# A two-block transformer layer on one core: squares read from PSUM by halves, the residual as one operation, and another order of work between the blocks

## The chip, the cores and the metric

The kernel runs on one core of one Trainium2 chip. The metric is the device time of one execution in microseconds (us), from runs of the whole program. Five engines work side by side, each through its own list of instructions in order: TensorE (PE, with its weight loads PEld), VectorE (DVE), ScalarE (ACT), GpSimd (POOL) and SyncE (SP, which here only issues DMA). They wait for each other on semaphores.

## The reference

Two blocks, one after the other, on 256 tokens of width 1024, in float32. The first is a hybrid attention layer, the second an attention layer with context and a mixture of experts. What the change touches is the seam between them:

```python
# end of the first block
m = jax.nn.sigmoid(gate_a) * (y_a @ w_a) + jax.nn.sigmoid(gate_b) * (y_b @ w_b)
return x + rms_norm(m @ w_o, norm_post)
...
# start of the second block: h is projected, hc is the context's
h = modulate(rmsnorm(x, norm_attn[l]), sh_a, sc_a)
hc = modulate(rmsnorm(xc, norm_attn[l]), csh_a, csc_a)
mix, mix_c = token_mixers(h, hc, rows, cols, w_in[l], ...)
```

`rms_norm` is y = x * rsqrt(mean(x * x) + 1e-6) times a gain. Inside `token_mixers`, h goes through w_in (1440 columns) and the compressed context through w_kv_up; then come attention, the router, and 16 experts whose weights are about half of all bytes read.

## The kernel before

**Data.** The tokens stand in two tiles of 128 (t = 0, 1), the width in halves of 512 (h = 0, 1). `xn` is the residual stream, `rn` holds rows (the output of w_o, later the normalised tokens), both 2 x 1024 columns.

**Groups.** The dense part of both blocks is a list of named groups, `DENSE` (line 96), and `schedule` (line 132) turns it into `SCHEDULE`, which PE, ACT and DVE each walk through in the same order. The name tells the work: `wo{t}{h}` is m @ w_o, `ckv{t}{h}` the context's keys and values, `hT{t}{h}` four transposes of normalised tokens, `xa{t}{h}` the projection by w_in (h = 2 is the last 416 columns), `bG`/`bF` spread a modulation row over all partitions, `modT2` turns the last modulation rows, `kc0` to `kc3` turn the context's keys, `lq`/`lk` turn the second block's latents.

**Two banks.** All these groups share two PSUM banks in turn (`BANK_OF`, line 109): a group gets the bank of the group two places ahead of it in the list, and PE waits at its start (`begin`, line 979) until ACT or DVE has released that bank (`leave`, line 513). So the order in the list also decides which copy PE waits for.

**Weights.** SP streams 2 MB slots of weights from HBM into the two halves of `ring` (and into `qk` for some), each when the previous user of the buffer is released (`released`, line 495). Float32 weights are split in a high part (ACT, line 650 through `copy`) and a low part (DVE, line 1724), in quarters: ACT waits until PE has finished with the same quarter of the weights before (`quarter_released`), DVE subtracts, PE starts. X2, X1, X0 are the thirds of w_in; `SPLIT_AFTER` (line 93) puts the four quarters of X2 behind hT01, modT2, bF1 and hT10.

**The seam.** For each `wo{t}{h}` ACT copies the bank to `rn`, which frees the bank. After the second half ACT squares and sums the row (`sum_squares`, line 655), DVE forms the mean, POOL raises it to the power -0.5 (line 952), DVE multiplies by root and gain (`block1_norm`, line 1601) and adds to `xn`. Then ACT squares `xn`, DVE and POOL form the second root and DVE writes the normalised tokens (`normalise`, line 1596), which `hT` turns. For t = 1 the squares of `xn` stand behind ckv11 on ACT, the rest behind hT01 on DVE.

## Time and profile before

| | us |
|---|---|
| median of 3 runs | 709.14 |
| lowest, highest | 708.98, 713.59 |
| the profiled execution | 711.06 |
| its span, first to last instruction | 709.3 |
| PE busy in it | 594.4 (84%) |
| DVE, ACT busy | 301.8, 225.8 |
| end of wo11 on PE (first block's last product) | 296.38 |
| start of xa02 (second block's first projection) | 317.50 |
| start of the second block's attention on PE | 376.09 |

The profiled execution is 1.9 us above the median. A row of the timeline gives start, duration, engine, line, operation, what it writes and reads, and in brackets how long its engine was idle before it and who ended that.

### The profile page before, as it was taken

Reading aid. Unit: us, or ns where it says so; the run is one execution under the profiler, and the core shown is the slowest. Engines: PE = TensorE matmul, PEld = TensorE weight load, DVE = VectorE, ACT = ScalarE, POOL = GpSimd, SP = SyncE. Lnnn points to the kernel's source line nnn. Section 1 sums busy time; section 2 is a strip of 40 time slices with the busy share of each in tenths; the row PEclk is TensorE's granted clock in tenths of the full one; section 3 lists DMA queues with packets and bytes.
Section 4 is the critical chain, followed back from the end, with each engine's and each line's share of the span. In section 5 each row is a group of like instructions: output and inputs, shape, how many; then the busy total and the mean of one; then the engine's idle time right before and its main releaser. Section 6 shows DMA issues by size and latency. Waiting matters only on the chain.

```text
span 709.3 us, 8571 instructions
## 1 busy us (share of the span) xinstructions
PE 594.4 (84%) x3373; PEld 366.7 (52%) x3373; DVE 301.8 (43%) x743; ACT 225.8 (32%) x485; POOL 17.6 (2%) x34
## 2 busy tenths in 40 slices
PE   3999999999998979969998999977995775656553
PEld 2998977778766748638654444436331311211011
DVE  5355576666664462473737876144210100000005
ACT  5244354445334233465235656111010100010001
POOL 3000000000000001000000000000000000000000
PEclk9999999999999999999999999996997798889787
DMA  8774867657688592355476001754899999999992
GB/s 320 258 254 151 326 237 280 267 215 290 262 328 347 237 369 106 118 179 207 147 305 260 1 1 66 290 201 185 335 430 426 426 424 430 427 427 428 423 414 90
DMA packets 19080, 193.00 MB, mean 272 GB/s; under 512 B 3296, under 2 KB 4576, under 8 KB 7264
## 3 DMA queue, kind: packets, MB, share of 16 engines
q1 hardware_dynamic: 15584, 188.49, 66.3%
q10 hardware_dynamic: 3168, 2.39, 1.1%
q0 software_dynamic: 288, 1.57, 0.5%
q8 instruction: 27, 0.44, 0.2%
q14 instruction: 13, 0.11, 0.0%
HBM read 190.87 MB, written 1.05 MB: 271 GB/s over the span
## 4 chain that ended last, share of the span: by engine, by line
PE 61%; DMA 24%; DVE 7%; ACT 3%; issue 2%; POOL 0%; SPq 0%; ACTq 0%; POOLq 0%; DVEq 0%
PE bank L1009 25%; DMA qk<-in_stream 17%; DMA ring<-in_stream 6%; PE bank L986 5%; PE bank L997 5%; PE bank L1495 3%; PE bank L1407 3%; PE bank L1253 3%; PE bank L1370 3%; PE bank L1338 2%; PE bank L1442 2%; PE bank L1335 2%; PE bank L1280 2%; DVE weight_parts L1724 2%; PE bank L1533 1%
## 5 line engine op out<-in xcount | busy, mean ns | idle before, releaser
L1009 PE MATMUL bank<-weight_parts,u_parts 128*128 128x512 f32 (+2 forms) x416 | 125.5, 384 | 3.7 <-ACT rows L650 1.2
L1724 DVE TENSOR_TENSOR weight_parts<-ring,weight_parts 128x1024 fp32r<-128x1024 f32 (+2 forms) x68 | 78.0, 1181 | 47.9 <-ACT weight_parts L650 45.8
L1009 PEld LDWEIGHTS bank<-weight_parts,u_parts 128*128 128x128 f32 x416 | 75.7, 188 | 20.9 <-issue 2.1
L650 ACT ACTIVATE weight_parts<-ring 128x1024 fp32r<-128x1024 f32 (+2 forms) x68 | 68.1, 1024 | 28.5 <-PE bank L1009 27.5
L1009 PE MATMUL bank<-u_parts,weight_parts 128*128 128x256 f32 x256 | 50.7, 293 | 4.6 <-DVE x_parts L1775 3.1
L1009 PE MATMUL bank<-weight_parts,x_parts 128*128 128x512 f32 (+1 forms) x128 | 48.3, 377 | 0.0
L1009 PEld LDWEIGHTS bank<-u_parts,weight_parts 128*128 128x128 f32 x256 | 42.0, 198 | 6.8 <-issue 4.7
L986 PEld LDWEIGHTS bank<-ident,sp 128*128 128x128 f32 (+1 forms) x218 | 26.1, 140 | 24.3 <-DVE sp L2016 15.7
L1009 PE MATMUL bank<-x_parts,weight_parts 128*128 128x256 f32 x128 | 37.0, 289 | 0.0
L986 PE MATMUL bank<-ident,sp 128*128 128x128 f32 (+1 forms) x218 | 32.1, 274 | 3.8 <-DVE sp L2016 1.9
L701 ACT ACTIVATE sp<-sp,small 128x128 f32<-128x128 f32 (+1 forms) x48 | 21.3, 444 | 35.8 <-DVE small L1685 35.8
L2123 DVE TENSOR_TENSOR sp<-sp,bank 128x512 f32<-128x512 f32 x4 | 2.8, 689 | 61.0 <-PE bank L1495 61.0
L2134 DVE COPY pt<-bank 128x512 f32<-128x512 f32 x4 | 2.8, 692 | 56.7 <-PE bank L1533 56.7
L1495 PE MATMUL bank<-ring,tz 128*32 128x512 f32 x128 | 19.9, 758 | 8.1 <-DMA ring<-in_stream 8.1
L2121 DVE SCALAR_TENSOR_TENSOR sp<-sp,bank 128x512 f32<-128x512 f32 x4 | 2.8, 688 | 55.9 <-ACT sp L916 55.9
L1009 PEld LDWEIGHTS bank<-weight_parts,x_parts 128*128 128x128 f32 x128 | 24.0, 188 | 4.5
L1495 PE MATMUL bank<-parts,tz 128*32 128x512 f32 x128 | 17.7, 682 | 10.1 <-DMA parts<-in_stream 10.1
L884 ACT ACTIVATE tz<-bank,small 128x128 f32<-128x128 f32 x16 | 6.0, 455 | 62.8 <-PE bank L1442 62.8
L1009 PEld LDWEIGHTS bank<-x_parts,weight_parts 128*128 128x128 f32 x128 | 25.3, 198 | 0.0
L650 ACT ACTIVATE mo<-bank 128x512 f32<-128x512 f32 (+3 forms) x22 | 12.0, 544 | 39.1 <-PE bank L1009 20.3
L650 ACT ACTIVATE pt<-bank 128x384 f32<-128x384 f32 (+1 forms) x18 | 9.2, 512 | 47.5 <-PE bank L1533 47.5
L997 PE MATMUL bank<-ring,lat 128*128 128x512 f32 (+2 forms) x56 | 23.0, 556 | 1.3 <-DVE tz L1593 0.8
(289 smaller groups left out, 994.7 us busy)
## 6 DMA issues: line engine op xcount, KB each, us to landing
ring<-in_stream SPq DMA_DIRECT2D x44, 2048.0 KB, 9.2
parts<-in_stream SPq DMA_DIRECT2D x12, 2048.0 KB, 35.5
qk<-in_stream SPq DMA_DIRECT2D x10, 2048.0 KB, 12.9
tabs<-in_stream SPq DMA_DIRECT2D x5, 2048.0 KB, 35.4
mo<-in_stream SPq DMA_DIRECT2D x5, 2048.0 KB, 38.6
vvc<-in_stream SPq DMA_DIRECT2D x5, 2048.0 KB, 39.2
tz<-in_stream SPq DMA_DIRECT2D x5, 1024.0 KB, 38.0
lat<-in_stream SPq DMA_DIRECT2D x5, 1024.0 KB, 40.1
```

What stands on the lines that cost most here:

```text
L650: ins = act.activation(dst, src, ACT.Copy, scale=scale)
L701: ins = act.activation(k, k, ACT.Exp, bias=nm[:, u % 2, 2 * b + q:2 * b + q + 1], accum_out=sums[:, u, 2 * b + q:2 * b + q + 1])
L986: return pe_.transpose(dst, src, ident[0:n, 0:n])
L997: ins = pe_.matmul(o, lhs(c), rhs(c), start=(c == 0), stop=(c == chunks - 1))
L1009: ins = pe_.matmul(o, lhs(a, c, i), rhs(b, c, i), start=(c == 0 and n == 0), stop=(c == chunks - 1 and n == 2))
L1253: ins = pe_.matmul(MB[32 * j:32 * j + 32, :], csil[:, c, :], w[:, k, 512 * j:512 * j + 512], start=(c == 0), stop=(c == KC - 1), tile_posi ...
L1280: pe_.matmul(SB[0][:, :], q[:, P:S], k.rearrange("p g s -> p (g s)"), start=True, stop=True)
L1335: ins = pe_.matmul(o, qwT[:, j, q * P:(q + 1) * P], kP[:, b, :], start=True, stop=True)
L1370: ins = pe_.matmul(OB[p % 2][HD * b:HD * b + HD, 0:S], v, pT[p % 2][:, b, i, :], start=(i == 0), stop=(i == 3), tile_position=(0, HD * b))
L1407: ins = pe_.matmul(D_(name)[:, :], oT[:, c, t * P:(t + 1) * P], w[:, c, :], start=(c == 0), stop=(c == KC - 1))
L1495: ins = pe_.matmul(bank[b][32 * e:32 * e + 32, :], xs[:, g % 2, c, e * CAP:(e + 1) * CAP], w[e][:, k, :], start=(c == 0), stop=(c == KC - ...
L1724: dve.tensor_tensor(quarter(weight_parts[:, SLOT:], name, q), quarter(slot(name), name, q), quarter(weight_parts, name, q).bitcast(F32), A ...
```

## The change

It does four things. (1) For each `wo{t}{h}`, ACT no longer copies: it squares and sums the half straight from PSUM (128x512), and DVE then multiplies the bank by the gain into `rn`, which now frees the bank (`post_gain`). (2) The root is applied together with the residual, one SCALAR_TENSOR_TENSOR for each half (`residual`), and the squares of `xn` are taken by halves. (3) The normalisation steps and the four quarters of X2's split become items of their own (`high`, `low`, `square`, `residual`, `mean`, `norm`) that the table `ACROSS` hangs behind wo01, wo11, ckv00 and ckv01. (4) The list is reordered: hT00, hT01 stand ahead of the ckv groups, hT10, hT11 right behind them, then xa02; the groups modT2, bG, bF and kc go in between the xa groups. A table of names replaces the counted squares. The instructions of PE are the same, in another order.

```diff
-SPLIT_AFTER = {"hT01": "X2", "modT2": "X2", "bF1": "X2", "hT10": "X2"}
...
-         "mT11", "modT1", "wo00", "cc0", "cc1", "wo10", "clT", "wo01", "wo11", "ckv00", "ckv01",
-         "ckv10", "hT00", "hT01", "ckv11", "bG0", "bG1", "modT2", "bF1", "bF0", "hT10", "hT11",
-         "kc0", "kc1", "kc3", "xa02", "kc2", "xa12", "xa01", "xa11", "xa00", "lq0", "lq1",
-         "xa10", "lk0", "lk1", "qu00", "qu01", "xkv00", "xkv01", "qwT0", "qu10", "qwT1", "kwT",
+         "mT11", "modT1", "wo00", "cc0", "cc1", "wo10", "clT", "wo01", "wo11", "hT00", "hT01",
+         "ckv00", "ckv01", "ckv10", "ckv11", "hT10", "hT11", "xa02", "kc0", "xa12", "modT2", "kc1",
+         "xa01", "bG0", "bG1", "xa11", "kc2", "bF1", "kc3", "bF0", "xa00", "lq0",
+         "xa10", "lq1", "lk0", "lk1", "qu00", "qu01", "xkv00", "xkv01", "qwT0", "qu10", "qwT1", "kwT",
...
+ACROSS = {"wo01": [("high", 0), ("residual", 0), ("square", 0), ("high", 1), ("mean", 0), ("low", 0), ("norm", 0)],
+          "wo11": [("high", 2), ("low", 1), ("residual", 1)], "ckv00": [("square", 1), ("mean", 1), ("low", 2), ("norm", 1)],
+          "ckv01": [("high", 3), ("low", 3)]}
...
+                elif kind == "high":
+
+                    arrived(eng, "X2")
+                    quarter_released(eng, X2_SPLIT - 1, n)
+                    copy(quarter(weight_parts, "X2", n), quarter(slot("X2"), "X2", n)).then_inc(split_a, 1)
+                elif kind == "square":
+                    for h in range(2):
+                        eng.wait_ge(x1_ready, 2 * n + h + 1)
+                        sum_squares(xn[:, n, 512 * h:512 * h + 512], 10 + n if h else 8 + n, sp[:, 0:512])
...
-                        copy(rn[:, t, 512 * h:512 * h + 512], D_(name)[:, :], name)
-                        if h == 1:
-                            kept(eng, f"wo{t}0")
-                            kept(eng, name)
-                            sum_squares(rn[:, t, :], 4 + t, sp[:, 0:D])
-                            if t == 0:
-
-                                eng.wait_ge(x1_ready, 1)
-                                sum_squares(xn[:, 0, :], 8, sp[:, 0:D])
+                        sum_squares(D_(name)[:, :], 14 + t if h else 4 + t, sp[:, 0:512])
...
-                        if name == "ckv11":
-                            eng.wait_ge(x1_ready, 2)
-                            sum_squares(xn[:, 1, :], 9, sp[:, 0:D])
...
-            def block1_norm(t):
-
-                mean_root(4 + t, 1, D, 5 + 2 * t)
+            def post_gain(t, h):
+
+                name = f"wo{t}{h}"
+                filled(eng, name)
                 eng.wait_ge(post_in, 16)
-                own(dve.scalar_tensor_tensor(rn[:, t, :], rn[:, t, :], rs[:, 4 + t:5 + t], post, ALU.mult, ALU.mult))
-                dve.tensor_tensor(xn[:, t, :], xn[:, t, :], rn[:, t, :], ALU.add).then_inc(x1_ready, 1)
-                eng.wait_ge(x1_ready, t + 1)
+                cols = slice(512 * h, 512 * h + 512)
+                eng.wait_ge(squares, squared(name))
+                leave(dve.tensor_tensor(rn[:, t, cols], D_(name)[:, :], post[:, cols], ALU.mult), name)
...
+                elif kind == "residual":
+                    eng.wait_ge(roots, n_mean[0])
+                    for h in range(2):
+                        kept(eng, f"wo{n}{h}")
+                        x = xn[:, n, 512 * h:512 * h + 512]
+                        dve.scalar_tensor_tensor(x, rn[:, n, 512 * h:512 * h + 512], rs[:, 14 + n:15 + n], x, ALU.mult, ALU.add)\
+                           .then_inc(x1_ready, 1)
+                elif kind == "mean":
+                    first_half(8 + n, squared(f"x{n}0"))
+                    half_mean(10 + n, 8 + n, squared(f"x{n}1"))
+                elif kind == "norm":
+                    eng.wait_ge(roots, n_mean[0])
+                    eng.wait_ge(x1_ready, 2 * n + 2)
+                    dve.tensor_scalar(rn[:, n, :], xn[:, n, :], rs[:, 10 + n:11 + n], None, ALU.mult).then_inc(normed, 1)
```

The first place is PE behind the last product of the first block, wo11. Names: rows are the tokens to turn (hT), `ring,lat` the context's products (ckv), `modr,lat` the spreads (bG, bF), `modr` alone modT2, `qk` the kc turns. Of the kernel before:

```order
L1009 MATMUL bank1<-weight_parts_64,ml_parts_67 128x512
L997 MATMUL bank0<-ring_49,lat_60 128x512 x2
L997 MATMUL bank1<-ring_49,lat_60 128x512 x2
L997 MATMUL bank0<-ring_49,lat_60 128x512 x2
L986 MATMUL bank1<-ident_61,rows_53 128x128 x4
L986 MATMUL bank0<-ident_61,rows_53 128x128 x4
L997 MATMUL bank1<-ring_49,lat_60 128x512 x2
L1183 MATMUL bank0<-modr_62,lat_60 128x512
L1183 MATMUL bank1<-modr_62,lat_60 128x512
L986 MATMUL bank0<-ident_61,modr_62 128x128 x4
L1183 MATMUL bank1<-modr_62,lat_60 128x512
L1183 MATMUL bank0<-modr_62,lat_60 128x512
```

Of the changed one, the same place on PE up to the first rows of xa02:

```order
L1017 MATMUL bank1<-weight_parts_64,ml_parts_67 128x512
L994 MATMUL bank0<-ident_61,rows_53 128x128 x4
L994 MATMUL bank1<-ident_61,rows_53 128x128 x4
L1005 MATMUL bank0<-ring_49,lat_60 128x512 x2
L1005 MATMUL bank1<-ring_49,lat_60 128x512 x2
L1005 MATMUL bank0<-ring_49,lat_60 128x512 x2
L1005 MATMUL bank1<-ring_49,lat_60 128x512 x2
L994 MATMUL bank0<-ident_61,rows_53 128x128 x4
L994 MATMUL bank1<-ident_61,rows_53 128x128 x4
L1017 MATMUL bank0<-weight_parts_64,u_parts_65 128x416 x2
```

The first ckv product now takes bank0 from hT00, where before it followed wo11 with a bank that had long been free, and the spreads and kc turns are gone from here.

The second place is PE at the end of xa12 and the start of xa01, in the changed kernel:

```order
L1017 MATMUL bank0<-weight_parts_64,u_parts_65 128x416 x2
L1017 MATMUL bank0<-weight_parts_64,hl_parts_68 128x416
L994 MATMUL bank1<-ident_61,modr_62 128x128 x4
L994 MATMUL bank0<-ident_61,qk_56 96x128 x4
L1017 MATMUL bank1<-weight_parts_64,u_parts_65 128x512 x2
```

and in the kernel before:

```order
L1009 MATMUL bank0<-weight_parts_64,u_parts_65 128x416 x2
L1009 MATMUL bank0<-weight_parts_64,hl_parts_68 128x416
L1009 MATMUL bank1<-weight_parts_64,u_parts_65 128x512 x2
L1009 MATMUL bank1<-weight_parts_64,hl_parts_68 128x512
L1009 MATMUL bank1<-weight_parts_64,u_parts_65 128x512 x2
```

Two short groups, modT2 and kc1, now stand between the two projections, and kc1 writes the bank that xa12 has just filled.

The third place is DVE over the first tokens, in the changed kernel, from the low parts of WO1 (the second weights of w_o) to the turned tokens (`weight_parts<-ring,weight_parts` with 2x416 columns is a quarter of X2):

```order
L1740 TENSOR_TENSOR weight_parts<-ring,weight_parts 128x1024 x4
L1616 TENSOR_TENSOR rows<-bank,vvc 128x512
...
L1751 SCALAR_TENSOR_TENSOR x_sb<-rows,small,x_sb 128x512 x2
L1581 TENSOR_SCALAR small<-small 128x1
L1621 SCALAR_TENSOR_TENSOR small<-small 128x1
L1744 TENSOR_TENSOR weight_parts<-ring,weight_parts 128x2x416
L1759 TENSOR_SCALAR rows<-x_sb,small 128x1024
L1616 TENSOR_TENSOR rows<-bank,vvc 128x512
L1621 SCALAR_TENSOR_TENSOR small<-small 128x1
L1744 TENSOR_TENSOR weight_parts<-ring,weight_parts 128x2x416
L1751 SCALAR_TENSOR_TENSOR x_sb<-rows,small,x_sb 128x512 x2
L1601 TENSOR_SCALAR tz<-bank,small 128x128 x4
```

The read that frees the bank of wo10 (L1616, the second row) stands behind four low parts, and the read that frees hT00's bank (L1601, the last) behind the whole step of wo11 and the second tokens' residual. Before, ACT freed the bank of wo10, and hT00's read stood behind the second tokens' addition in the same way, but three ckv groups ran on PE ahead of it.

## Rows read from the trace of the kernel before

**Rows 1.** The page, part 4: shares of the chain that ended last.
```profile
PE 61%; DMA 24%; DVE 7%; ACT 3%; issue 2%; POOL 0%; SPq 0%; ACTq 0%; POOLq 0%; DVEq 0%
```

**Rows 2.** Sums by stretch: busy us of each engine, PE's granted clock, DMA share, GB/s.
```profile
285.18:296.38 11.20, 11.20 (x49) 9.28 (x50) 4.57 (x8) 1.89 (x4) 0.56 (x1) 1.00 0.50 187
296.38:317.50 21.12, 15.79 (x56) 7.17 (x56) 15.61 (x30) 16.22 (x34) 1.65 (x3) 1.00 0.38 134
317.50:376.09 58.59, 54.83 (x243) 40.54 (x244) 26.82 (x61) 22.15 (x41) 1.40 (x2) 1.00 0.60 233
376.09:498.62 122.53, 112.07 (x520) 58.29 (x523) 73.04 (x231) 50.69 (x136) 1.11 (x2) 0.94 0.34 132
498.62:694.23 195.61, 132.52 (x888) 41.04 (x880) 13.06 (x26) 11.94 (x25) 0.00 (x0) 0.86 1.00 419
311.50:317.50 6.00, 2.96 (x21) 1.98 (x20) 5.85 (x12) 4.20 (x9) 0.00 (x0) 1.00 0.59 202
```

**Rows 3.** The timeline at the start of wo01, by engine.
```profile
280.96 4.94 DVE L1724 TENSOR_TENSOR weight_parts<-ring,weight_parts 128x1024 fp32r<-128x1024 f32 x4
284.55 0.58 ACT L650 ACTIVATE rows<-bank 128x512 f32<-128x512 f32 x1
285.18 0.73 PE L1009 MATMUL bank<-weight_parts,u_parts 128*128 128x512 f32 x2 [1.19 <-ACT rows L650]
```

**Rows 4.** The chain at the second block's residual: a half read from PSUM, a half squared.
```profile
473.66 0.70 DVE rows L2068
475.11 0.73 ACT sp L661 x2
```

**Rows 5.** The timeline of POOL and DVE, steps of the seam.
```profile
293.07 0.56 POOL L952 TENSOR_TENSOR small<-small 128x1 f32<-128x1 f32 x1 [10.36 <-DVE small L1566]
293.66 1.28 DVE L1605 SCALAR_TENSOR_TENSOR rows<-rows,small,vvc 128x1024 f32<-128x1024 f32 x1 [0.67 <-POOL small L952]
298.32 0.75 DVE L1599 TENSOR_SCALAR rows<-x_sb,small 128x1024 f32<-128x1024 f32 x1 [0.67 <-POOL small L952]
302.53 1.37 DVE L1593 TENSOR_SCALAR tz<-bank,small 128x128 f32<-128x128 f32 x4
309.24 1.02 DVE L1724 TENSOR_TENSOR weight_parts<-ring,weight_parts 128x832 fp32r<-128x832 f32 x1
```

**Rows 6.** SP's timeline and the DMA view: X2's issue, KB, us to landing.
```profile
285.93 0.33 SPq L613 DMA_DIRECT2D ring<-in_stream  x1
ring<-in_stream SPq DMA_DIRECT2D x1, 2048.0 KB, 7.6
```

**Rows 7.** The chain and the timeline of PE: ckv00 to ckv10, bG0 with bG1, modT2.
```profile
296.38 5.32 PE bank L997 x12
305.77 2.15 PE L1183 MATMUL bank<-modr,lat 128*128 128x512 f32 x4
308.35 0.63 PE L986 MATMUL bank<-ident,modr 128*128 128x128 f32 x4 [0.43 <-ACT vvc L650]
```

**Rows 8.** The timeline of ACT and DVE around the splits of X1 and X0.
```profile
324.42 4.40 ACT L650 ACTIVATE weight_parts<-ring 128x1024 fp32r<-128x1024 f32 x4 [1.09 <-PE bank L1009]
328.73 0.50 ACT L650 ACTIVATE mo<-bank 128x416 f32<-128x416 f32 x1
333.87 0.29 DVE L1615 TENSOR_TENSOR sp<-mo,lat 128x128 f32<-128x128 f32 x1 [3.72 <-ACT mo L650]
337.37 4.62 DVE L1724 TENSOR_TENSOR weight_parts<-ring,weight_parts 128x1024 fp32r<-128x1024 f32 x4
340.26 0.53 ACT L661 ACTIVATE pt<-mo 128x384 f32<-128x384 f32 x1
```

**Rows 9.** Who PE waited for from xa02 to the attention: us in total, times, longest.
```profile
PE bank L986 <- DVE mo L1647: 0.8, 1, 0.8
```

**Rows 10.** Sums by stretch around a fall of the clock, columns as in rows 2.
```profile
473.55:477.24 3.69, 0.00 (x1) 0.00 (x1) 2.09 (x5) 0.72 (x2) 0.56 (x1) 1.00 0.75 222
478.00:479.00 1.00, 0.85 (x4) 0.45 (x3) 0.96 (x3) 0.11 (x1) 0.00 (x0) 0.50 1.11 475
```

More of the change, by code:

```diff
@@ L127, with squared @@
     ["qb0", "qb1", "kb0", "kb1", "vb0", "vb1", "za0", "za1", "zb0", "zb1", "gA00", "gA10", "gA01", "gA11"])}
+X2_SPLIT = SPLIT.index("X2")
+ACROSS = {"wo01": [("high", 0), ("residual", 0), ("square", 0), ("high", 1), ("mean", 0), ("low", 0), ("norm", 0)],
+          "wo11": [("high", 2), ("low", 1), ("residual", 1)], "ckv00": [("square", 1), ("mean", 1), ("low", 2), ("norm", 1)],
+          "ckv01": [("high", 3), ("low", 3)]}
+SQUARES = ["x0", "x1", "wo00", "cc0", "cc1", "wo10", "wo01", "x00", "x01", "wo11", "x10", "x11", "q0", "kv0", "q1", "kv1",
+           "ou00", "ou01", "ou10", "ou11", "f00", "f01", "f10", "f11"]
+def squared(name):
+    return SQUARES.index(name) + 1
 def schedule():
@@ L134, in schedule @@
         for k in range(1, len(SPLIT)):
-            if LAST_USE[SPLIT[k - 1]] == name and SPLIT[k] not in SPLIT_AFTER.values():
+            if LAST_USE[SPLIT[k - 1]] == name and SPLIT[k] != "X2":
                 out += [("split", (k, q)) for q in range(4)]
@@ L140, in schedule @@
             out += [("split", (0, q)) for q in range(4) if (q == 0) == (name == "xT10")]
-        if name in SPLIT_AFTER:
-            k = SPLIT.index(SPLIT_AFTER[name])
-            out.append(("split", (k, sum(i == ("split", (k, q)) for i in out for q in range(4)))))
+        out += ACROSS.get(name, [])
         if name in MOD_AFTER:
@@ L947, in _ @@
             eng.wait_ge(zeroed, 1)
-            for n, (k, w) in enumerate([(0, 1), (1, 1), (2, 2), (6, 2), (4, 1), (8, 1), (5, 1), (9, 1), (10, 2), (12, 2),
+            for n, (k, w) in enumerate([(0, 1), (1, 1), (2, 2), (6, 2), (14, 1), (10, 1), (15, 1), (11, 1), (10, 2), (12, 2),
                                         (14, 1), (15, 1), (4, 1), (5, 1)]):
@@ L1639, in late_x @@
                 i = 10 + 2 * t
-                eng.wait_ge(squares, i)
+                eng.wait_ge(squares, squared(f"kv{t}"))
                 dve.tensor_scalar(ss[:, i:i + 1], ss[:, i:i + 1], 1.0 / QR, EPS, ALU.mult, ALU.add)
@@ L1725, in _ @@
                                       quarter(weight_parts, name, q).bitcast(F32), ALU.subtract).then_inc(split_v, 1)
+                elif kind == "low":
+                    eng.wait_ge(split_a, 4 * X2_SPLIT + n + 1)
+                    dve.tensor_tensor(quarter(weight_parts[:, SLOT:], "X2", n), quarter(slot("X2"), "X2", n),
+                                      quarter(weight_parts, "X2", n).bitcast(F32), ALU.subtract).then_inc(split_v, 1)
+                elif kind == "residual":
[12 more added lines that the diff above has]
+                    dve.tensor_scalar(rn[:, n, :], xn[:, n, :], rs[:, 10 + n:11 + n], None, ALU.mult).then_inc(normed, 1)
                 elif kind == "score":
@@ L1929, in _ @@
                         ins.then_inc(cat_ready, 1)
-                    elif name[:2] == "wo" and name[3] == "1":
-                        t = int(name[2])
-                        block1_norm(t)
-                        if t == 0:
-                            normalise(0, 8, 6)
+                    elif name[:2] == "wo":
+                        t, h = int(name[2]), int(name[3])
+                        post_gain(t, h)
+                        if h == 0:
+                            first_half(4 + t, squared(name))
+                        else:
+                            half_mean(14 + t, 4 + t, squared(name))
                     elif name[:2] == "hT":
@@ L1948, in _ @@
                            .then_inc(h_ready, 1)
-                        if name == "hT01":
-                            normalise(1, 8, 8)
                     elif name in ("xa01", "xa11"):
@@ L2063, in _ @@
                     if h == 1:
-                        first_half(t, 13 + 2 * t)
+                        first_half(t, squared(f"ou{t}0"))
                     filled(eng, name)
```

13 lines of the change are left out of this document (9 added, 4 removed).

## The prediction

> **What bounds the kernel now.** First the page's shares of the chain that ended last [rows 1]: PE has 61% of it, DMA 24%. The sums by stretch tell where [rows 2]. In the last 195.6 us the DMA share is 1.00 at 419 GB/s: the experts' weights stream back to back, up to 694.2. In the 122.5 us ahead of it the DMA share is only 0.34: the buffers are full and SP waits until PE has used the first expert's weights. So nothing behind the seam takes up a shift: if PE enters the attention x us later than 376.09, the stream starts x later and the kernel ends x later. I count every us at PE's entry into the attention as a us of the whole.
>
> Up to there PE is the engine to watch. From the start of wo01 it is busy for 11.20 of 11.20 us, then 15.79 of 21.12 between wo11 and xa02, then 54.83 of 58.59 up to the attention [rows 2]. The change does not touch PE's instructions, only their order, so the time can change by PE's waits alone: 5.33 us in the seam, 3.76 us behind it, and 1.19 us ahead of wo01 [rows 2, 3]. That is the ledger: at most 5.33 us are to be had in the seam, and each group moved out of it is paid for in full where it goes, with whatever wait it brings.
>
> **Step 1: the start of wo01.** PE waits for the bank of wo10, which ACT's copy frees at 284.55 + 0.58 = 285.13 [rows 3]. In the changed kernel ACT squares it from PSUM first. No row shows that: the copy of as many columns is 0.58, the square of a half with its accumulator 0.73 [rows 3, 4], so 0.58 to 0.73, about 0.7, to 285.3. Then DVE has to multiply, and DVE is busy with the four low parts of WO1 until 280.96 + 4.94 = 285.90. A half read from PSUM takes 0.70 [rows 4], so the bank is free at about 286.55 and wo01 starts at 286.6: **+1.4**. The square is hidden behind the low parts, so its price does not enter. wo01 and wo11 still take 11.2 and end at 297.8.
>
> **Step 2: the seam.** Behind wo01 (done 292.2): square 0.7, gain 0.7, mean 0.15, root 0.56 with 0.1 on each side, residual in two halves. One pass of a SCALAR_TENSOR_TENSOR over 1024 is 1.28 [rows 5], so 0.66 a half; the separate addition, 1.2, is gone. `xn` is ready at 295.9, its second square ends at 296.8, the second root at 297.6; DVE spends that root on a low part of X2 (1.02 by the row, about 0.94 to the next start), so the normalisation of 0.75 ends at 298.65. hT00 starts at 298.8, **1.0** behind wo11. X2 must be there for ACT's first high part: issued at 285.93 and landed 7.6 later, at 293.5 [rows 6], when ACT arrives at 293.0. ACT then ends it at 294.4, and its next square is not due before 295.3, so this half us is covered.
>
> hT01 follows at 299.5 to 300.1. Then comes ckv00, whose bank is hT00's. DVE reads that bank only behind its own list: gain of wo11 (to 299.35), mean, a low part (to 300.45), the two halves of the second residual (to 301.8), then four reads of 1.37 in all [rows 5]: 303.15. ckv00 starts at 303.3, a wait of **3.2**. In the old order ckv groups ran here with free banks. The four ckv groups follow without a wait at 1.76 each (three take 5.32 [rows 7]), to 310.3. The second tokens' squares, mean, root and normalisation lie under them (done about 309.1), hT10 and hT11 take 0.63 each with 0.2 between, and xa02 waits **0.75** for DVE's 1.37 over hT10's bank: it starts at 312.5. The low parts of X2 end at 310.0 and are hidden. The waits here sum to 1.0 + 0.1 + 3.2 + 0.2 + 0.75 = 5.2, against 5.3 before: **-0.1**. So the seam gets shorter, 14.7 us instead of 21.1, but nearly all of it by moved work: three kc turns (0.55 each), modT2 (0.63), four spreads (1.07 each) [rows 7], 6.5 us.
>
> **Step 3: the moved groups among the xa groups.** Before, a projection of 5.45 us stood between two short ones and hid the copies. Now short groups follow each other, and each needs the bank of the group two places ahead. Six waits, each from the end of the group that starts it; 0.1 is PE's start behind a release.
> - kc1 needs xa12's bank. ACT first makes the last high part of X1, which itself waits for xa12's end (4.40 for four, 1.1), then copies 0.50 [rows 8]: 1.6. PE has only modT2, 0.63: wait **1.1**.
> - xa01 needs modT2's bank, read by DVE behind the last low part of X1 (4.62 for four, 1.15 [rows 8]): 1.1 + 1.15 + 0.25 = 2.5 behind xa12, where PE arrives at 2.3: **0.4**.
> - xa11 needs bG0's: ACT copies xa01 (0.58), squares the two latents (0.53 for the larger [rows 8], about 1.05 for both), copies bG0 (0.56): 2.3 against two spreads, 2.15: **0.3**.
> - bF1 needs xa11's: again a last high part, 1.05, and a copy, 0.6, against kc2's 0.55: **1.25**.
> - kc3 needs kc2's, behind the latents' squares and a copy of 0.57: 3.4 behind xa11, PE arrives at 2.9: **0.6**.
> - xa00 needs kc3's, which DVE copies behind its last low part (2.25 behind xa11), the rotation, mean, root and scaling of the second latents (333.87 to 337.37, 3.5 us with its root [rows 8]) and 0.64 for itself: 6.4. PE has 5.1 us of work and waits up to there: **1.35**.
>
> Sum 5.0. Against that, lq1 no longer waits 0.8 for the second latents [rows 9], while hops of 0.3 in all come by at the lk and qu groups: about -0.5. Step 3: **+4.5**. X1 is issued at ckv11's end (310.3) and, at the 7.6 of X2 [rows 6], there at 317.9, before its first quarter is free at 319.0.
>
> **The sum.** +1.4 - 0.1 + 4.5 = +5.8, less 0.1 for rounding: **+5.7**. The profiled execution would be 711.06 + 5.7 = 716.8; against the median of 709.14, 1.9 us lower than it, I predict **714.8**. Bounds: if the six waits are each 0.3 us shorter or longer (a hop between engines, 1.8 in all), 713.0 and 716.6.
>
> **The rivals.**
> - *The clock falls between the blocks.* In the changed kernel PE has from 297.8 to 303.3 only two sets of transposes, 1.3 us, and at a stretch 3.2 us of nothing. The row that speaks for it: behind 3.69 us without PE work the granted clock goes from 1.00 to 0.50, from 2.4 to 1.2 GHz, while PE turns tiles [rows 10]. Against it: in 311.50 to 317.50 PE did transposes alone, half of the time, and the clock stayed at 1.00 [rows 2]; and 3.2 is shorter than 3.69. The Trainium skill, TensorE: Matmul & The Clock Gate, Part 4: PE-mode transpose, says that transposes do not count as PE-busy in the same way. By that rule the fall would be near certain here; the stretch of transposes at 1.00 does not bear it out. The price: the 122.5 us at a mean of 0.94 hold 0.06 x 2 x 122.5 = 14.7 us at the low level [rows 2]; if one fall is a third of that, some 5 us, of ckv work at half speed, it costs 2.5: +8.2, **717.3**, slower by 1.2%. It decides if ckv00's products run at twice their time. This is the case on the slower side.
> - *The six waits of step 3 are not there*, since ACT's copies come ahead of the splits or PE holds its work: +1.4 - 0.1 - 0.5 = +0.8, **709.9**. Against it: before, the copy of xa02's partner stands right behind the fourth high part, at 328.73 [rows 8].
> - *The seam hides its waits too*, what the edits say on their face: hT00 on time and ckv00 not held: 0.8 - 4.2 = -3.4, **705.7**. Against it: DVE's list in front of hT00's read.
> - *More waits*: X1 later than 319.0, or DVE behind by a us more in the seam, as each us there is a us of the end: +7 to +8, **716.5**.
>
> **How the numbers follow.** The sum as worked out 0.50, the clock 0.25, longer waits 0.10, no waits in step 3 0.12, a gain 0.03. The likeliest gives 714.8. For 8 in 10 I leave out the gain, part of the second rival and the tail of the clock: **711.0 to 718.5**. About 1% is what a measurement of this kernel can tell from no change: 702.1 and 716.2. Faster 0.03; slower the clock and most of the longer waits, 0.33; within it 0.64.
>
> **What would show it.** wo01 starting 1.4 us after its bank's copy did, behind DVE L1616. PE idle for about 3 us ahead of the first ckv rows, released by DVE's tz rows. xa02 at about 312.5 and the attention at about 381.9. Waits of about 1 us ahead of kc1, bF1 and xa00. The forecast is wrong if PE's waits from wo01 to the attention do not sum to about 16 us (10.3 before), or if the granted clock is below 1.00 there.

## The result and the profile after

The changed kernel takes 720.93 us (median; 720.54 to 726.08), the kernel before, beside it, 710.32 (708.98 to 713.59): a ratio of 1.0151, 95% interval 1.0118 to 1.0184. Forecast were 714.8 us and at most 718.5. The direction was right and the size was not: it lost 10.6 us, where the sum said 5.7. (The forecast started from 709.14, the median of before at that time; 1.2 us of the 6.1 between 714.8 and 720.93 are the other base.)

The profiled executions, 711.06 and 720.54 us, are 9.5 us apart. The stretch from clT's end (283.99 before, 283.14 after) to kx3's end, where the attention begins, tells it best: **92.10 us before, 103.58 after, +11.48**. (The changed kernel was 0.85 us ahead at clT's end and took 1.2 us less behind kx3, hence 9.5.) Sums by stretch of the changed kernel, columns as in [rows 2]: the wait ahead of wo01; wo01 with wo11; the seam; the four ckv groups in it; xa02 to the attention; the experts' stream.

```profile
283.14:285.71 2.57, 0.01 (x1) 0.00 (x0) 2.44 (x4) 1.24 (x3) 0.00 (x0) 0.95 0.00 0
285.71:298.36 12.65, 12.64 (x48) 10.00 (x48) 4.33 (x12) 3.83 (x8) 1.03 (x2) 0.87 0.45 166
298.36:316.13 17.77, 11.71 (x34) 5.62 (x33) 11.52 (x24) 8.80 (x23) 3.33 (x3) 0.81 0.08 17
304.83:314.18 9.35, 9.35 (x18) 4.09 (x19) 4.54 (x8) 4.09 (x11) 1.26 (x1) 0.76 0.00 0
316.13:386.72 70.59, 61.85 (x267) 43.40 (x268) 30.07 (x68) 26.51 (x51) 1.40 (x2) 1.00 0.59 229
508.00:703.60 195.60, 132.37 (x888) 40.91 (x880) 13.01 (x26) 11.95 (x25) 0.00 (x0) 0.86 1.00 419
```

The chain that ended last, as in [rows 1], hardly changed:

```profile
PE 62%; DMA 23%; DVE 8%; ACT 3%; issue 2%; POOL 1%; SPq 0%; ACTq 0%; POOLq 0%; DVEq 0%
```

In the sums the column to read is the granted clock, third from the end. Before, it was 1.00 in all stretches up to the attention [rows 2]. Now wo01 and wo11 run at a mean of 0.87 and take 12.65 us instead of 11.20, and the ckv groups run at 0.76 and take 9.35 where four at the 1.76 of before [rows 7] make about 7.05 (the runs with the clock held, below, took 7.11). The last row is that of before: 195.60 us at 419 GB/s. From kx3's end to the end of the program it is 333.2 us before, 332.0 after, and 331.9 to 333.4 in every run below, with entries between 371.0 and 391.6. So, to within 1.5 us, a us at PE's entry to the attention is a us of the whole.

Who PE waited for from clT to kx3 (us in total, times, longest), the largest:

```profile
PE bank L1005 <- DVE tz L1601: 3.5, 1, 3.5
PE bank L1017 <- DVE rows L1616: 2.6, 1, 2.6
PE bank L994 <- DVE rows L1759: 1.6, 1, 1.6
PE bank L994 <- ACT mo L660: 1.6, 2, 1.1
PE bank L1017 <- DVE tabs L2009: 1.5, 1, 1.5
PE bank L1191 <- ACT mo L660: 1.3, 1, 1.3
```

They are, in this order, ckv00, wo01, hT00, kc1 (1.12 of the 1.6; the other 0.45 stands at 362.3, behind xa10), xa00 and bF1: the places that steps 1 to 3 name. Their lengths were forecast as 3.2, 2.6 (1.19 as before, and 1.4), 1.0, 1.1, 1.35 and 1.25.

The waits over 0.1 us sum to 10.07 us before and 17.24 after. So the +11.48 is made of:

| | forecast | measured |
|---|---|---|
| the wait ahead of wo01 | +1.4 | +1.38 |
| the clock, in wo01 and wo11 | 0 | +1.45 |
| waits in the seam | -0.1 | +0.73 |
| the clock, in ckv00 to ckv11 | 0 (a rival) | +2.30 |
| waits behind xa02 | +4.5 | +5.06 |
| rest, mostly three overlaps of 0.16 between groups that three more waits cut | 0 | +0.56 |

Why +0.73 in the seam, and not the -0.1 of the forecast? hT00 waits 0.64 longer than forecast and ckv00 0.3, and most of this is GpSimd's root. The timeline of POOL and DVE in the changed kernel, in the order of time:

```profile
294.62 0.56 POOL L960 TENSOR_TENSOR small<-small 128x1 f32<-128x1 f32 x1 [12.73 <-DVE small L1621]
297.72 1.02 DVE L1744 TENSOR_TENSOR weight_parts<-ring,weight_parts 128x832 fp32r<-128x832 f32 x1
297.89 1.27 POOL L960 TENSOR_TENSOR small<-small 128x1 f32<-128x1 f32 x1 [2.71 <-DVE small L1621]
299.19 0.75 DVE L1759 TENSOR_SCALAR rows<-x_sb,small 128x1024 f32<-128x1024 f32 x1 [0.45 <-POOL small L960]
300.69 1.26 POOL L960 TENSOR_TENSOR small<-small 128x1 f32<-128x1 f32 x1 [1.53 <-DVE small L1621]
```

The root at 294.62, with nothing beside it on DVE, takes 0.56, as before [rows 5]. The one at 297.89 begins 0.17 us into a low part of X2 and takes 1.27. DVE's norm 0 starts at 299.19, 0.45 us behind the end of the low part; the residual of wo11 (301.99) starts 0.44 us late in the same way. The low part that was to fill the wait for the root made the root late.

When did the clock fall? In the wait ahead of ckv00, which began at 301.33:

```profile
301.33:302.50 1.17, 0.00 (x0) 0.00 (x0) 0.73 (x2) 1.14 (x4) 0.62 (x1) 1.00 0.00 0
302.50:304.83 2.33, 0.00 (x1) 0.03 (x1) 2.30 (x7) 1.00 (x3) 0.00 (x0) 0.51 0.00 0
```

It was at 0.5 from 302.5 to 309.4, so the fall came 1.2 us into this wait, and the 3.5 us of the whole wait don't explain it. Ahead of it PE had stood still for 1.64 us and turned tiles for 1.3 us. The fall at wo01 began 0.25 us before the wait ended and lasted to 288.9.

### The profile page after: what moved, and what is told of

Read it like the earlier page. It is cut to its first block, busy times and chain, and to the rows that moved or that the text cites. A ratio compares the mean times of both kernels' runs of the same rounds, so it can differ in the third digit from the quotient of the medians.

```text
span 718.7 us, 8598 instructions
## 1 busy us (share of the span) xinstructions
PE 597.7 (83%) x3373; PEld 367.7 (51%) x3373; DVE 302.7 (42%) x751; ACT 225.0 (31%) x489; POOL 19.8 (3%) x34
## 4 chain that ended last, share of the span: by engine, by line
PE 62%; DMA 23%; DVE 8%; ACT 3%; issue 2%; POOL 1%; SPq 0%; ACTq 0%; POOLq 0%; DVEq 0%
PE bank L1017 26%; DMA qk<-in_stream 17%; PE bank L1005 5%; PE bank L994 5%; DMA ring<-in_stream 5%; PE bank L1503 3%; PE bank L1415 3%; PE bank L1261 3%; PE bank L1378 3%; PE bank L1346 2%; DVE weight_parts L1740 2%; PE bank L1343 2%; PE bank L1450 2%; PE bank L1288 2%; PE bank L1541 1%
## 5 line engine op out<-in xcount | busy, mean ns | idle before, releaser
L1740 DVE TENSOR_TENSOR weight_parts<-ring,weight_parts 128x1024 fp32r<-128x1024 f32 (+1 forms) x64 | 74.2, 1193 | 46.7 <-ACT weight_parts L660 44.4
L1005 PE MATMUL bank<-ring,lat 128*128 128x512 f32 (+2 forms) x56 | 24.9, 598 | 4.2 <-DVE tz L1601 3.5
L960 POOL TENSOR_TENSOR small<-small 128x1 f32<-128x1 f32 (+1 forms) x14 | 10.5, 750 | 572.2 <-DVE small L1586 364.2
```

What stands on the lines that cost most here:

```text
L1005: ins = pe_.matmul(o, lhs(c), rhs(c), start=(c == 0), stop=(c == chunks - 1))
L1740: dve.tensor_tensor(quarter(weight_parts[:, SLOT:], name, q), quarter(slot(name), name, q), quarter(weight_parts, name, q).bitcast(F32), A ...
```

## The experiments

All are compared by medians and by the stretch from clT's end to kx3's end in their profiled execution. Between executions of one kernel the time varies by up to 8 us, more than most of these effects; the seventh experiment shows why. The stretch is the finer measure, but it is one execution for each kernel. By their medians (721.67, 722.23, 719.52 and 720.83 us) the first four runs, with wo10's copy, the two fillings and the moved groups, can't be told from the changed kernel (720.93); the runs with two causes taken away, or with the old order, can.

**1. wo10's bank by ACT's copy.** The changed kernel with this edit undone:

```
+ if name == "wo10":
+     copy(rn[:, t, cols], D_(name)[:, :], name)      # frees the bank
+     sum_squares(rn[:, t, cols], ...)
+ ...DVE: rn = rn * post in place, instead of D_("wo10") * post
```

> The changed kernel, with one of its edits undone: bank wo10 is copied out by ACT and freed by that copy, as before, and its squares and its gain go by the copy in SBUF; wo00, wo01 and wo11 stay as changed. Theory A (the freeing of the bank by a VectorE gain behind four low parts costs TensorE 1.4 us, and this longer wait is what lets the clock fall for 3.4 us in wo01, 1.45 us): the wait ahead of wo01 is 1.2 us instead of 2.57, wo01 and wo11 take 11.2 us instead of 12.65 at a granted clock of 1.00, and the kernel is 2.5 to 2.9 us faster than the changed one (ratio to the kernel before about 1.011). Rival B (the clock falls there for another cause, such as the work of ACT and VectorE at its side): only the wait is shorter, 1.4 us, and the clock still falls. Rival C (what is won in wo01 is given back at hT00 and ckv00, because the residual's chain on ACT, VectorE and GpSimd sets them and not TensorE): ckv00 starts no earlier than 19.5 us after wo01's start in the changed kernel, and the time stays within 0.5 us of the changed kernel's.

Its rows, the same stretches as above (wait; wo01 and wo11; seam; xa02 on):

```profile
283.49:284.68 1.19, 0.00 (x0) 0.00 (x0) 1.06 (x2) 1.16 (x3) 0.00 (x0) 1.00 0.00 0
284.68:295.88 11.20, 11.20 (x48) 8.93 (x48) 5.36 (x14) 3.93 (x10) 0.56 (x1) 1.00 0.52 187
295.88:313.85 17.97, 11.38 (x32) 5.54 (x33) 12.05 (x24) 9.06 (x24) 3.81 (x3) 0.81 0.08 15
313.85:386.29 72.44, 64.65 (x267) 45.03 (x268) 30.05 (x68) 26.52 (x51) 1.40 (x2) 0.95 0.58 224
```

The wait is 1.19, the clock holds in wo01, and xa02 starts 30.36 us behind clT instead of 32.99: -2.63, theory A as far as wo01 goes (2.83 less 0.2, by which the seam is longer: 17.97 us for 17.77). Rival C is out. But another fall came later, where none was in the changed kernel: xa02 on at 0.95, 72.44 us instead of 70.59. It began behind the waits ahead of bF1 and kc3; PE was busy 2.8 us longer, and xa00's wait, 0.56 instead of 1.52, hid 1.0 of that. The fall took 1.85 back, the stretch is 102.80 us in all, and the time of this run, 721.67 us (ratio 1.0136, 1.0081 to 1.0191), shows nothing of the gain. That this second fall is caused by the edit I can't say. The same fall, at the same place and of the same size, stands in the run with the low parts moved (below), which has no fall in wo01 either; the waits in front of it are the same in the changed kernel, where the clock held.

**2 and 3. Idle work in the waits.** The changed kernel with matmuls that nothing reads, once products and once transposes:

```
+ def filler(count):
+     ...
+     for i in range(count):
+         pe.matmul(SB[0], ident, lat[:, 0:512])      # or: turn(SB[0][:, 0:P], ident)
  def dense(name):
+     filler({"wo01": 2, "hT00": 1, "ckv00": 3}.get(name, 0))      # or 16, 8, 24 turns
```

> The changed kernel plus idle matmuls that nothing reads: matrix products of 512 columns in FP32 (about 1.07 us each) into a free bank, two in TensorE's wait ahead of wo01, one ahead of hT00 and three ahead of ckv00. No wait of the kernel is taken away. Theory A (the clock falls because TensorE stands still in these waits, and the falls cost 1.45 us in wo01 and wo11 and 2.3 us in ckv00 to ckv11): the granted clock stays at 1.00 from wo01 to xa02, wo01 and wo11 take 11.2 us, the four ckv groups 7.0 us, and the kernel is 3 to 3.8 us faster than the changed one although TensorE does more work (ratio to the kernel before about 1.010). Rival B (the groups are slower by contention or the clock falls by heat or power): times of the groups as in the changed kernel, and the kernel no faster. Rival C (the clock is kept, but TensorE was ahead of its partners, so that waits take the place of what was won): clock 1.00, the waits behind ckv longer by up to 2.3 us, time within 1.5 us of the changed kernel's.

> As the run before it, but the filling work is transposes of a 128 x 128 tile (about 0.12 us each) instead of matrix products: 16 ahead of wo01, 8 ahead of hT00, 24 ahead of ckv00, some 1.9, 1 and 2.9 us of them. Theory A (any work of TensorE keeps the clock up): as the run with products, 3 to 3.8 us faster than the changed kernel, granted clock 1.00. Rival B (transposes don't count as work for the clock gate, as the Trainium skill has it in TensorE: Matmul & The Clock Gate, Part 4: PE-mode transpose): the clock falls as in the changed kernel or for longer, wo01 and wo11 12.6 us or more, ckv 9.4 us or more, and the kernel is as slow as the changed one. The same rival would say of the changed kernel that hT00 and hT01, 16 transposes between two waits, are part of what lets the clock fall before ckv00.

With products, then with transposes: wo01 and wo11; the ckv groups; the whole stretch.

```profile
290.87:302.04 11.17, 11.17 (x49) 9.27 (x50) 4.32 (x11) 3.83 (x8) 1.04 (x2) 1.00 0.51 188
308.50:315.61 7.11, 7.11 (x18) 3.23 (x19) 4.25 (x8) 3.98 (x11) 1.27 (x1) 1.00 0.00 0
288.29:388.08 99.79, 87.59 (x360) 58.90 (x359) 48.33 (x105) 40.26 (x83) 5.76 (x6) 1.00 0.49 186
```
```profile
285.99:297.16 11.17, 11.17 (x50) 9.22 (x51) 4.32 (x12) 3.83 (x8) 1.04 (x2) 1.00 0.51 188
303.62:310.73 7.11, 7.11 (x18) 3.23 (x19) 4.25 (x8) 3.97 (x11) 1.26 (x1) 1.00 0.00 0
283.41:383.40 99.99, 87.65 (x395) 62.14 (x394) 48.33 (x105) 40.11 (x83) 5.76 (x6) 1.00 0.48 186
```

PE does more and is done earlier: 99.8 and 100.0 us instead of 103.6, at the full clock, 2.4 GHz, throughout. That is 3.8 and 3.6 us for the two falls, the 1.45 and 2.3 of the table. The waits were no shorter (wo01 again starts 2.58 us behind clT), so it is the clock, and it fell because PE stood still. Over all runs here, the clock fell at wo01 in three of four executions with this wait left empty and in none of three with it filled, and in the ckv groups in four of four and in none of three. Transposes hold it as well as products do. The Trainium skill, TensorE: Matmul & The Clock Gate, Part 4: PE-mode transpose, has it that transposes don't count as PE-busy in the same way; in these waits they kept the clock as products did, and rival B of the second run falls. In time the two are 1.0130 (1.0076 to 1.0185) and 1.0100 (1.0042 to 1.0158) of the kernel before. By time alone the one with products (722.23 us) would be no gain at all: its profiled execution reached clT 4.9 us later than the one with transposes, at 288.29, by falls ahead of the stretch.

**4. The moved groups put back.** One table changed, from ckv11 on:

```
- "ckv11", "hT10", "hT11", "xa02", "kc0", "xa12", "modT2", "kc1", "xa01", "bG0", "bG1", "xa11", "kc2", "bF1", "kc3", "bF0", "xa00", "lq0", "xa10", "lq1",
+ "ckv11", "bG0", "bG1", "modT2", "bF1", "bF0", "hT10", "hT11", "kc0", "kc1", "kc3", "xa02", "kc2", "xa12", "xa01", "xa11", "xa00", "lq0", "lq1", "xa10",
```

> The changed kernel with one table changed: bG0, bG1, modT2, bF1 and bF0 stand again behind ckv11, kc0, kc1 and kc3 ahead of xa02, and kc2, xa12, xa01, xa11, xa00, lq0, lq1, xa10 as before; the order from wo01 to ckv11, the split of X2 and all other edits stay as changed. Theory A (the moved groups meet six waits of 5.0 us on ACT and VectorE between xa02 and lk0, where they had covered the split of X2 and most of these steps before): the waits at kc1, xa01, xa11, bF1 and xa00 are gone, waits of about 0.8, 0.3 and 0.6 at kc0, kc1 and kc3 and 0.2 at xa02 stand in their place, and the kernel is 3 to 3.5 us faster than the changed one (ratio about 1.010). Rival B (the waits there cost nothing, since the arrival of X1 or of X0 bounds xa01 and xa00 anyway): the same time as the changed kernel, within 1 us, with the idle time at xa01 or xa00. Rival C (a longer stretch of short groups at half clock): the clock stays at half longer than 6.8 us behind ckv00, and up to 1.5 us of the gain is lost.

The seam, and xa02 on:

```profile
298.69:324.33 25.64, 18.16 (x58) 8.63 (x57) 14.38 (x31) 13.36 (x31) 3.32 (x3) 0.87 0.34 133
324.33:382.91 58.58, 54.83 (x243) 40.51 (x244) 26.80 (x61) 22.16 (x41) 1.40 (x2) 1.00 0.58 223
```

From xa02 on PE is busy 54.83 of 58.58 us, as before [rows 2], with waits of 3.57 where the changed kernel had 8.65. In the seam the waits rise from 6.1 to 7.5. The stretch is 99.55 us, 4.0 less than in the changed kernel. Theory A, a little larger than the 3 to 3.5 I expected. The time is 1.0111 (1.0054 to 1.0168) of the kernel before.

**5. The new steps in the old order.** The tables of before, all new operations kept:

```
- ACROSS = {"wo01": [("high", 0), ("residual", 0), ...], ...}      and DENSE as changed
+ ACROSS = {"wo01": [("residual", 0), ("square", 0), ("mean", 0), ("norm", 0)], "wo11": [("residual", 1)],
+           "ckv00": [("square", 1), ("mean", 1), ("norm", 1)], "hT01": [("high", 0), ("low", 0)],
+           "modT2": [("high", 1), ("low", 1)], "bF1": [("high", 2), ("low", 2)], "hT10": [("high", 3), ("low", 3)]}      and DENSE as before
```

> All the new steps of the change (squares from PSUM by halves, gain out of PSUM, residual in one operation by halves) in the order of before: TensorE's groups, the quarters of X2 and the place of the second tokens' norm behind ckv11 are as they were. Read from clT's end to kx3's end, which is 92.1 us in the kernel before, 103.6 in the changed kernel and 99.6 in the run with the groups moved back behind ckv11. Theory A (the steps cost only at bank wo10, the order costs the rest): the wait ahead of wo01 is 2.6 us instead of 1.19, with the clock's fall behind it wo01 and wo11 take 12.65 us instead of 11.20, all waits behind are as before to 0.5 us in sum; 95 us, and the kernel 2 to 3 us slower than before (ratio 1.003 to 1.005). Rival B (the halves themselves, seven more operations on ACT and VectorE, load the seam): waits of 2 us or more at ckv11, modT2, hT11 and kc0 besides, 97 us or more, ratio 1.007 or more. Rival C (the shorter chain saves as much as wo10's bank costs): 92 us, ratio 1.000.

And then with wo10's bank freed by ACT's copy as well:

> The run with the new steps in the order of before, and wo10's bank freed by ACT's copy besides, as before: of the change only the squares from PSUM (of wo00, wo01 and wo11), the gain out of PSUM, the residual in one operation by halves and the halves of the squares are left. That run took 94.5 us from clT's end to kx3's end, with a wait of 2.57 us ahead of wo01 and a fall of the clock behind it (12.76 us for wo01 and wo11), and was 1.0038 of the kernel before. Theory A (wo10's bank is all that the new steps cost): wait 1.19, wo01 and wo11 11.2 us, 91.5 to 92 us in the stretch, ratio 0.998 to 1.000. Rival B (the new steps cost elsewhere as well): 93 us or more, ratio above 1.002. Rival C (the shorter chain of the residual gives something once wo10 is out of the way): under 91 us, ratio under 0.998; by the waits of the run in the order of before, which stand at ckv11, modT2, hT11, kc0 and xa02 as they did, I don't expect it.

The seam and the whole stretch of each:

```profile
302.74:323.34 20.60, 15.73 (x57) 7.29 (x56) 15.21 (x31) 14.70 (x33) 1.18 (x3) 1.00 0.39 139
287.41:381.93 94.52, 83.34 (x347) 58.23 (x348) 48.23 (x105) 40.22 (x83) 3.61 (x6) 0.98 0.52 197
```
```profile
295.45:316.04 20.59, 16.84 (x56) 8.14 (x56) 15.20 (x31) 14.83 (x33) 1.17 (x3) 0.92 0.40 138
283.08:374.71 91.63, 82.96 (x347) 58.04 (x348) 48.41 (x105) 41.01 (x84) 3.61 (x6) 0.98 0.54 202
```

94.5 and 91.6 us against 92.1 before, and 1.0038 (1.0012 to 1.0065) and 1.0002 (0.9978 to 1.0027) in time. So the shorter chain of squares, gain and residual gives 0.5 us in this order (the seam takes 20.6 instead of 21.12), too little for the times to show, and bank wo10 is all that the new steps cost: 2.9 us, half a wait and half the clock. The order cost the rest, 9.1 us of the stretch (103.58 against 94.52). The second seam also shows that a fall isn't always paid: there the clock fell behind the wait ahead of kc0, PE was busy 1.1 us longer, and the waits at the next two groups were shorter by as much.

**6. Are the costs additive?** The moved groups back, and the filling transposes:

> Two runs put together: bG, modT2, bF, kc0, kc1 and kc3 back in their places of before, behind ckv11, and the filling transposes ahead of wo01 (16), hT00 (8) and ckv00 (24). Theory A (the waits behind xa02 and the clock's two falls are separate costs that add up): from clT's end to kx3's end 103.6 - 4.0 - 3.6 = 96.0 us, granted clock 1.00 up to kx3's end but for falls that come anywhere; the kernel about 7 us faster than the changed one (ratio to before 1.005). Rival B (one hides the other: with the clock up, TensorE comes to its partners earlier and waits longer): 98 us or more.

```profile
286.22:381.79 95.57, 87.00 (x395) 62.18 (x394) 47.96 (x105) 40.47 (x83) 5.75 (x6) 1.00 0.51 195
```

95.6 where 96.0 was expected, and 1.0059 (1.0032 to 1.0087) in time: they add up, and this time the medians show it too (716.75 us; 1.0151 for the changed kernel). What is left above 92.1 is the wait ahead of wo01 and those at hT00 and ckv00.

**The root of GpSimd.** Each low part one step later:

```
- "wo01": [..., ("mean", 0), ("low", 0), ("norm", 0)], "wo11": [("high", 2), ("low", 1), ("residual", 1)], "ckv00": [..., ("mean", 1), ("low", 2), ("norm", 1)]
+ "wo01": [..., ("mean", 0), ("norm", 0), ("low", 0)], "wo11": [("high", 2), ("residual", 1), ("low", 1)], "ckv00": [..., ("mean", 1), ("norm", 1), ("low", 2)]
```

> The changed kernel with three low parts of X2 put one step later in VectorE's order: low part 0 behind norm 0, low part 1 behind residual 1, low part 2 behind norm 1, so that VectorE does nothing while GpSimd takes the root. Theory A (GpSimd's root takes 1.27 us instead of 0.56 us because VectorE's low part of a weight quarter runs beside it): all roots of the seam take 0.56 to 0.6 us. Rival B (the root takes longer because it finds two columns of one in another state, or because its first instruction behind a long rest is slow): they stay at 1.27 us. For the time: hT00 then starts 0.3 to 0.7 us earlier, but the low parts push the freeing of wo11's bank and the second tokens' steps back, by my count 1 us at hT01 and 0.7 us more at ckv00, so that xa02 starts 0 to 1.4 us later than in the changed kernel.

The roots of the second square and of wo11:

```profile
300.69 0.56 POOL L960 TENSOR_TENSOR small<-small 128x1 f32<-128x1 f32 x1 [2.71 <-DVE small L1621]
303.72 0.55 POOL L960 TENSOR_TENSOR small<-small 128x1 f32<-128x1 f32 x1 [2.47 <-DVE small L1621]
```

All four take 0.55 to 0.56: theory A. Nothing was changed on POOL, only what DVE does beside it. The Trainium skill, SBUF — State Buffer, Who interferes with whom, says that a VectorE instruction with two SBUF inputs contends with a GpSimd instruction that reads SBUF, that the shared port pair is an exclusive lock, and that issue order decides who blocks. The rows of the changed kernel agree: the low part began first, and the root at 297.89 ends 0.42 us behind the low part's end (298.74). It was no gain all the same: hT00 starts 0.92 us behind wo11 instead of 1.64, but hT01 now waits 0.97 and ckv00 3.7, and xa02 starts 31.72 us behind clT. That is 0.2 us more than the changed kernel without its fall in wo01, which this execution doesn't have:

```profile
287.40:289.97 2.57, 0.00 (x1) 0.00 (x1) 2.44 (x4) 1.23 (x3) 0.00 (x0) 1.00 0.00 0
289.97:301.17 11.20, 11.20 (x48) 8.93 (x48) 3.77 (x11) 3.83 (x8) 1.04 (x2) 1.00 0.50 187
```

The same wait of 2.57 us ahead of wo01, and no fall behind it. The changed kernel and the runs with the groups moved back and with the new steps in the old order had one. A wait of this length makes a fall possible and not certain. (One execution, 726.63 us, with falls ahead of wo01 and behind xa02.)

**7. A kernel that beats both.** If the end goes by PE's waits, and the durations are known, a better order can be looked for on paper: with each group's duration and what each step waits for. The rule of the order found is that every step of the residual's chain has a group or two with a free bank beside it. wo10's bank goes by ACT's copy.

```
  "clT", "wo01", "wo11", "ckv00", "ckv01", "bG0", "hT00", "ckv10", "hT01", "ckv11", "bG1", "kc0", "modT2", "kc1", "hT10", "bF1",
  "hT11", "xa02", "xa12", "xa01", "xa11", "xa00", "xa10", "bF0", "lq0", "lq1", "kc3", "lk0", "lk1", "kc2", "qu00", ...
+ ACROSS = {"wo01": [("residual", 0), ("high", 0), ("square", 0), ("mean", 0)], "wo11": [("high", 1)],
+   "ckv00": [("high", 2), ("residual", 1)], "ckv01": [("norm", 0)], "bG0": [("square", 1), ("low", 0)],
+   "hT00": [("mean", 1), ("low", 1)], "ckv11": [("norm", 1)], "bF1": [("low", 2), ("high", 3), ("low", 3)]}
```

> A kernel meant to beat both: the new steps of the change with wo10's bank freed by ACT's copy, and another order in which ckv00, ckv01 and bG0 stand between wo11 and hT00, ckv10 between hT00 and hT01, ckv11, bG1, kc0, modT2 and kc1 between hT01 and hT10, bF1 between hT10 and hT11, and kc2, kc3 and bF0 among xa00 to lk1; X2's high parts behind wo01, wo11, ckv00 and hT11's neighbours in the same manner. Every step of the residual's chain then has one or two groups of TensorE beside it. Theory A (all that the order costs or gives lies in TensorE's waits in this stretch): by the durations of the traces the waits between clT and kx3 fall from 10.3 to about 5.5 us, 87 to 88 us from clT's end to kx3's end (92.1 before), clock at 1.00, and the kernel 3 to 5 us faster than before (ratio 0.993 to 0.996). Rival B (GpSimd's roots at 1.27 us beside VectorE's parts, and other stretchings that the durations don't hold, fill the new gaps up again): 91 us or more, ratio 0.998 or above. Rival C (X1's load starts with ckv11's end, which is later here, and xa01 waits for it): idle time of over 1 us ahead of xa01.

```profile
301.66:317.06 15.40, 14.27 (x51) 6.47 (x50) 11.71 (x27) 10.73 (x26) 2.11 (x3) 1.00 0.29 106
289.29:376.41 87.12, 81.76 (x348) 56.99 (x348) 48.16 (x105) 41.07 (x84) 4.32 (x6) 1.00 0.57 213
```

The seam is 15.40 us with PE busy for 14.27 of them, and the stretch 87.12 instead of 92.10, for the same 81.8 us of PE's work. 707.05 us against 711.40, ratio 0.9943 (0.9917 to 0.9970). Theory A: the waits are 5.4 us, where 5.5 were expected, and the rivals fall. (One root took 1.26 us beside a low part, at 309.76, but PE waited for nothing behind it.) Whether it needs the change's new steps or would gain as much with the old ones wasn't tried.

That execution reached clT at 289.29, 5 us later than the kernel before, and ended only 0.7 us ahead of it. Its clock had fallen ahead of the stretch, at 223.6, 261.2 and 268.0, behind the waits at cxT10 and gB01, at modulation slot 11, and behind two of 0.8 us after that. The kernel before had waits of 1.12, 0.89, 2.26, 1.07 and 0.90 us at the same places and a clock of 1.00. So transposes were put into these waits too, and both kernels were run side by side:

> The interleaved kernel that was 0.9943 of the kernel before, with idle transposes (about 0.12 us each, into a free bank, read by nothing) in TensorE's waits ahead of it and in it: 7 ahead of cxT10, 5 ahead of gB01, 17 ahead of modulation slot 11, 7 ahead of mT01, 5 ahead of modT1 and 8 ahead of wo01. Theory A (the spread of several us between executions of every kernel here comes from falls of the clock at about 223 and 261 to 268 us of the span, behind the waits of 1.1 and 0.9 us ahead of cxT10 and gB01 and of 2.3 to 2.4 us ahead of slot 11; wo10 and clT end at 283.1 to 284.0 us in executions without and at 286.2 to 289.3 us in executions with such falls): clT ends at 283 to 284 us with the clock at 1.00 up to there, the times of all executions lie within 2 to 3 us, and the median is 1 to 3 us below the interleaved kernel's, ratio 0.989 to 0.993. Rival B (the falls come by power, heat or a window that the transposes don't count in): falls at the same places as often, median as the interleaved kernel's. Rival C (the transposes are issued late or run at half clock and delay what stands behind them): the groups behind them start 0.2 us or more later each, and the kernel is up to 1 us slower.

> The interleaved kernel a second time, beside the one with transposes on the same chip: ratio 0.992 to 0.997 of the kernel before, as the first time; the comparison with transposes is read between these two.

Without the transposes (the first time), and with them: 217 to 245 us; 257 us to clT's end.

```profile
216.94:245.00 28.06, 26.05 (x130) 18.85 (x130) 11.30 (x16) 10.26 (x17) 0.00 (x0) 0.94 0.63 243
257.00:289.29 32.29, 28.20 (x124) 20.30 (x122) 13.86 (x21) 10.18 (x18) 2.99 (x7) 0.89 0.48 197
```
```profile
216.00:245.00 29.00, 28.31 (x153) 20.85 (x152) 11.78 (x18) 10.52 (x18) 0.00 (x0) 1.00 0.70 275
256.00:283.91 27.91, 27.03 (x149) 20.96 (x148) 12.38 (x20) 9.26 (x17) 2.98 (x7) 1.00 0.51 209
```

The clock stays at 1.00 up to clT. The six executions with transposes lie between 704.44 and 705.29 us; the eight beside them without lie between 704.72 and 710.31, and the nineteen of the kernel before between 709.00 and 717.09. The medians are 705.16 (ratio 0.9890, 0.9859 to 0.9920), 706.25 (0.9915, 0.9881 to 0.9949) and 712.87. So the transposes gain 1 us in the median, the low end of what was expected (the intervals of the two ratios overlap), and nearly all of the spread; the lowest times of the two hardly differ. Rival B falls. Against rival C stands clT's end at 283.91, inside the 283.1 to 284.0 of executions without falls.

## Why the prediction was wrong

- **What bounds the kernel, and the ledger.** Half right. That a us at PE's entry is a us of the end held in all profiled runs. "The time can change by PE's waits alone", since PE's instructions are the same, is the step that failed: it took PE's durations as fixed. A wait can have two prices, its own length and the clock behind it. The second was 3.75 us of the 11.48, and filling the waits took 3.6 to 3.8 us away.
- **Step 1.** Right in cause, place and size (2.57 us behind DVE's low parts; 2.6 forecast). What it left out is that this wait could also bring the clock down, +1.45; the rival on the clock looked only at the waits in front of ckv00.
- **Step 2.** The mechanism was right, both waits stand where they were put (ckv00 3.5 for 3.2). hT00's was mis-sized, 1.64 for 1.0: the root was taken at 0.56 from a row in which DVE was idle, and in the new order DVE works beside it, 1.27. That made DVE's next step 0.45 us late at hT00 and 0.44 ahead of ckv00. The experiment with the low parts moved shows the cause; the other 0.2 us at hT00 I haven't followed.
- **Step 3.** Right. In the changed kernel kc1 1.12 (1.1), xa01 0.46 (0.4), xa11 0.48 (0.3), bF1 1.29 (1.25), kc3 0.48 (0.6), xa00 1.52 (1.35): 5.35 us for 5.0, and +5.06 net for +4.5. Putting the groups back gave 4.0 us.
- **The clock's rival.** This fall happened, in place (ckv00 to ckv11) and in size (2.3 us for 2.5), though the time went past the 717.3 of this rival too, since it had only one of the two falls. It had a chance of 0.25. The argument against it, that 3.2 us is less than the 3.69 of [rows 10], read one fall as if it were a bound: that row shows that 3.69 is enough, not that less is safe. The fall came 1.2 us into the wait, behind the wait of 1.64 ahead of hT00 and 1.3 us of transposes.
- **The range.** It reached to 718.5 and left out the tail of the clock's case. With both falls among its cases (5.7 + 1.45 + 2.3 = 9.5, 718.6) and the root's 0.9 it would have reached to 719.5, still 1.4 us under the median measured; 1.2 of that is the base, 710.32 beside the changed kernel instead of 709.14.
- **What would show it.** The text had set waits of about 16 us and a granted clock of 1.00 as its tests. The waits sum to 17.2; the clock is 0.87 and 0.76, and this test was the one to tell.

What stays open: why the same wait ahead of wo01 brings a fall in the executions of three kernels and not in that of a fourth, why the clock fell behind bF1 in two executions and held in the others with the same waits, and the 0.56 us of rest, of which only the cut overlaps were read from rows.

## What to carry to other kernels

A wait of TensorE that lets its clock fall is paid twice, unless waits behind it take the slower work up: put it among the prices of a reordering, in each place where a wait grows or two waits come close together. If such a wait can't be taken away, transposes into a free bank keep the clock, cost nothing inside the wait, and here took most of the spread out of the measurement as well. And work that fills an engine's wait for another engine must not slow that other one: a VectorE operation with two SBUF inputs beside GpSimd's root made the root the later of the two. (Moving that operation away wasn't a gain here, since it then stood ahead of other steps.)

## What was not expected of the hardware

- The clock fell behind a single wait of 2.57 us (mean 0.87 over the 12.65 us that followed), in three of four traced executions with this wait left empty, and never behind one of 1.19 at the same place.
- The clock fell 1.2 us into the wait ahead of ckv00, behind another wait of 1.64 us and 1.3 us of transposes.
- Transposes alone, 16, 8 and 24 of them in waits of 2.6, 1.6 and 3.5 us, kept it at 1.00, as products did.
- A GpSimd operation on 128x1 took 1.27 instead of 0.56 us beside a VectorE operation that reads two SBUF operands.
- The work up to clT's end, the same in all kernels here but for wo00 and wo10, ended between 283.1 and 289.3 us of the profiled executions, by falls of the clock behind waits of 0.8 to 2.4 us; with these waits filled, the times of six executions of one kernel lay within 0.85 us.
